# Turnings of attention rows, norm steps, spare banks and gates placed anew in a chain of two fused networks

## What is computed

```python
def rmsnorm(x, g):
    return x * rsqrt(mean(x * x, axis=-1) + EPS) * g

# mix: 8 heads of 64, 512 rows in blocks of 128
s = einsum('bhqd,bkhd->bhqk', q_i, k) * scale + cq_i[..., None] - c[:, :, None, :]
p = softmax(where(mask, s, -inf), axis=-1)
y_att = einsum('bhqk,bkhd->bqhd', p, v)
x = x + concat([rmsnorm(y_conv, g_conv_out), rmsnorm(y_att, g_att_out)]) @ w_mix_out

# x: 4 heads of 256, 256 memory rows
q = rmsnorm(x, g_xattn) @ w_q
k, v = split(rmsnorm(mem, g_mem) @ w_kv, 2)
x = x + attention(q, k, v) @ w_o

# last stage: 16 heads of 64
z = einsum('bhqd,bhsd->bhqs', q, k) * scale
suffix = cumsum(log_sigmoid(-z) * mask, axis=3, reverse=True) - log_sigmoid(-z) * mask
a = where(mask, exp(log_sigmoid(z) + suffix), 0)
o = einsum('bhqs,bshe->bhqe', a, v)
x = x + (o * silu(g)) @ w_out
```

## Time and profile before

| | us |
|---|---|
| median of 3 runs | 2913.24 |
| lowest and highest | 2910.73, 2915.46 |
| profiled execution | 2911.05 |
| its span | 2909.2 |
| PE busy | 2843.3 |
| DVE busy | 1676.3 |
| ACT busy | 1092.2 |
| POOL busy | 397.3 |
| mean granted clock of PE | 0.995 |

### The profile page before, as it was taken

How to read it: one execution, slowest core, us unless ns; L and a number is a source line. 1 busy time by engine, 2 the same in 40 slices (tenths; PEclk the granted TensorE clock), 3 DMA queues, 4 the chain that set the end, 5 groups by cost and what they waited for, 6 DMA issues and landing times.

```text
span 2909.2 us, 34967 instructions
## 1 busy us (share of the span) xinstructions
PE 2843.3 (98%) x14241; PEld 2363.5 (81%) x14241; DVE 1676.3 (58%) x2400; ACT 1092.2 (38%) x1699; POOL 397.3 (14%) x263
## 2 busy tenths in 40 slices
PE   8999999999999999999999999999999899899988
PEld 7888887888888888888887889888888787678777
DVE  5554357675464533555247776555533677768884
ACT  4322244554332322323234454422222444444442
POOL 2000111110100001000011220100001322154430
PEclk9999999999999999999999999999999999999999
DMA  4332332243233233332323233233323222131211
GB/s 141 101 95 94 95 88 73 66 127 106 87 94 97 88 101 98 101 95 87 105 71 92 68 108 118 80 109 95 101 91 98 70 64 69 47 88 59 72 59 51
DMA packets 302240, 258.08 MB, mean 89 GB/s; under 512 B 11367, under 2 KB 299904, under 8 KB 302080
## 3 DMA queue, kind: packets, MB, share of 16 engines
q1 hardware_dynamic: 300704, 254.76, 28.7%
q10 hardware_dynamic: 1024, 1.05, 0.2%
q0 software_dynamic: 352, 0.03, 0.0%
HBM read 252.66 MB, written 2.10 MB: 88 GB/s over the span
## 4 chain that ended last, share of the span: by engine, by line
PE 82%; DVE 10%; ACT 3%; issue 3%; POOL 2%; DMA 1%; ACTq 0%; SPq 0%; POOLq 0%; DVEq 0%
PE PS L1525 26%; PE PS L1527 25%; PE PS L1526 25%; DVE WL L2255 3%; PE PS L1531 2%; PE PS L1770 1%; DVE AF L2701 1%; DVE SM L2619 1%; ACT AF L2129 0%; PE PS L1623 0%; PE PS L1812 0%; PE PS L1811 0%; DVE AR L2711 0%; ACT WH L1872 0%; POOL SM L2869 0%
## 5 line engine op out<-in xcount | busy, mean ns | idle before, releaser
L2255 DVE TENSOR_TENSOR WL<-RAW,WH 128x1024 fp32r<-128x1024 f32 x480 | 617.9, 1293 | 572.9 <-ACT WH L1872 572.6
L1525 PE MATMUL PS<-XH,WL 128*128 128x512 f32 x2256 | 904.4, 401 | 2.9 <-DVE XL L2265 2.9
L1527 PE MATMUL PS<-XH,WH 128*128 128x512 f32 x2256 | 883.3, 392 | 0.0
L1526 PE MATMUL PS<-XL,WH 128*128 128x512 f32 x2256 | 882.1, 391 | 0.0
L1872 ACT ACTIVATE WH<-RAW 128x1024 fp32r<-128x1024 f32 x448 | 465.4, 1044 | 1005.9 <-PE PS L1527 994.6
L1525 PEld LDWEIGHTS PS<-XH,WL 128*128 128x128 f32 x2256 | 425.8, 189 | 101.5 <-issue 12.7
L1527 PEld LDWEIGHTS PS<-XH,WH 128*128 128x128 f32 x2256 | 425.2, 188 | 91.5
L1526 PEld LDWEIGHTS PS<-XL,WH 128*128 128x128 f32 x2256 | 426.3, 189 | 81.1
L1525 PE MATMUL PS<-AR,WL 128*128 128x512 f32 (+1 forms) x1216 | 465.3, 383 | 7.3 <-DVE SC L2599 3.5
L1527 PE MATMUL PS<-AR,WH 128*128 128x512 f32 (+1 forms) x1216 | 460.7, 379 | 0.0
L1526 PE MATMUL PS<-AR,WH 128*128 128x512 f32 (+1 forms) x1216 | 460.6, 379 | 0.0
(11 more groups left out here) (259 smaller groups left out, 3000.0 us busy)
## 6 DMA issues: line engine op xcount, KB each, us to landing
RAW<-in_w_ffn_gu_dram SPq DMA_DIRECT2D x176, 512.0 KB, 3.5
RAW<-in_w_ffn_down_dram SPq DMA_DIRECT2D x80, 512.0 KB, 3.4
RAW<-in_w_mix_in_dram SPq DMA_DIRECT2D x48, 512.0 KB, 4.0
RAW<-in_w_xkv_dram SPq DMA_DIRECT2D x32, 512.0 KB, 3.4
RAW<-in_a_w_in_dram SPq DMA_DIRECT2D x32, 512.0 KB, 4.2
RAW<-in_w_mix_out_dram SPq DMA_DIRECT2D x16, 512.0 KB, 3.4
RAW<-in_w_xq_dram SPq DMA_DIRECT2D x16, 512.0 KB, 4.1
RAW<-in_w_xo_dram SPq DMA_DIRECT2D x16, 512.0 KB, 3.4
```

The source lines that it names most:

```text
L1525: pe.matmul(o, ll, rh, start=start, stop=False, skip_group_check=skip)
L1526: pe.matmul(o, lh, rl, start=False, stop=False, skip_group_check=skip)
L1527: return pe.matmul(o, lh, rh, start=False, stop=stop, skip_group_check=skip)
L2255: dve.tensor_tensor(l, raw_slot(n), F(h), ALU.subtract).then_inc(sg["wl"].up(n))
```

## The change

Four things are placed anew; no arithmetic changes.

1. *Rows.* In `att` of mix and of the last stage there is no break between the turning of a row and the scores that follow it, as long as there are scores (n < 16, n < 32). The rates of the side streams are lower accordingly, as they now count fewer and larger steps.
2. *Mix.* The second half of the first values goes to bank 7 instead of the next in turn.
3. *x.* `norm_a` stands behind 12 steps of the first queries' tile instead of 10, `norm_b` behind 5 steps of the second keys instead of 2. The output projection takes its first two pairs of banks in the order in which they come in turn.
4. *Last stage.* `norm_a` stands 3 steps into the tile q1, `norm_b` 3 steps into k1, which gets a bank of its own and is finished before the rows start. Gate 6 moves from `opening` into block t=7.

```diff
@@ mix, att @@
                     self.add("bt", (s, m), "ptr", "ph")
-                    yield
+                    if n >= 16:
+                        yield
@@ mix @@
-        self.drain(self.flow(self.values(s, 0)))
+        self.drain(self.flow(self.values(s, 0, 7)))
-        side = self.stream(att(0, 4), 6.5 / 64)
+        side = self.stream(att(0, 4), 4.3 / 64)
-            side = self.stream(att(4 * m, 4 * m + 4), 10.5 / 80)
+            side = self.stream(att(4 * m, 4 * m + 4), 6.3 / 80)
-        side = self.stream(att(12, 16), 10.5 / 80)
+        side = self.stream(att(12, 16), 6.3 / 80)
-        side = self.stream(att(16, 19), 4.5 / 44)
+        side = self.stream(att(16, 19), 4.4 / 54)
@@ x, second_keys @@
-            for _ in range(2):
+            for _ in range(5):
                 yield next(g)
             self.norm_b(s)
@@ x @@
         g = self.flow(queries(0))
-        for _ in range(10):
+        for _ in range(12):
             next(g)
         self.norm_a(s)
...
+        a, b, c, d = self.turn
         self.own_banks(4, 5)
-        self.out_proj(s, self.stream(att(3), 8.2 / 48), flow=True)
+        self.out_proj(s, self.stream(att(3), 8.2 / 48), ((a, b), (c, d)), flow=True)
@@ out_proj @@
-        ch = {p: out(p, 2 * p) for p in range(4)}
+        ch = {p: out(p, bb) for p, bb in enumerate((*pairs, (4, 5), (6, 7)))}
@@ values @@
-            b = self.take()
+            b = self.take() if spare is None or n == 0 else spare
@@ last stage, att @@
                     self.later(5, "btl", (s, m), "pl")
-                    yield
+                    if n >= 32:
+                        yield
@@ last stage @@
+        g = self.tile(q1, b1)
+        for _ in range(3):
+            next(g)
         self.norm_a(s)
-        g = self.tile(q1, b1)
-        for _ in range(6):
+        self.drain(g)
+        kb = self.take()
+        g = self.tile(((s, "k1"), 0), kb)
+        for _ in range(3):
             next(g)
         self.norm_b(s)
-        self.drain(g)
...
-        side = self.stream(att(0, 4), 6 / 64)
-        self.weave(self.flow(self.chain(qk("k", 1), self.values(s, 0), gated(0))), side)
+        self.drain(self.flow(g))
+        self.give(kb, "bql", (s, "k", 1))
+        self.heads_in(s, "k", 1)
+        side = self.stream(att(0, 4), 4.3 / 48)
+        self.weave(self.flow(self.chain(self.values(s, 0), gated(0))), side)
...
-            if t < 7:
-                main.append(gated(t - 1))
-            side = self.stream(att(4 * t - 4, 4 * t), 10.5 / (32 + (32 if t % 2 else 0) + (16 if t < 7 else 0)))
+            main.append(gated(t - 1))
+            side = self.stream(att(4 * t - 4, 4 * t), 6.3 / (48 + (32 if t % 2 else 0)))
...
-            yield from self.chain(gated(6), gated(7))
+            yield from gated(7)
             yield from self.mm(out[0], range(0, 6))
-        side = self.stream(att(28, 33), 13 / 56)
+        side = self.stream(att(28, 33), 8.2 / 40)
```

More of the change, by code:

```diff
@@ L758, in xattn, with out_proj @@
             self.finish(side)
+        a, b, c, d = self.turn
         self.own_banks(4, 5)
-        self.out_proj(s, self.stream(att(3), 8.2 / 48), flow=True)
-    def out_proj(self, s, side, flow=False):
+        self.out_proj(s, self.stream(att(3), 8.2 / 48), ((a, b), (c, d)), flow=True)
+    def out_proj(self, s, side, pairs, flow=False):
         def out(p, bb):
-            return self.chunk((s, f"o{p}"), (bb, bb + 1), "o", [("x", (s + 1, 2 * p + c)) for c in range(2)])
+            return self.chunk((s, f"o{p}"), bb, "o", [("x", (s + 1, 2 * p + c)) for c in range(2)])
         def close(p):
             self.resid(s, (2 * p, 2 * p + 1), ((ch[p], 0), (ch[p], 1)))
-        ch = {p: out(p, 2 * p) for p in range(4)}
+        ch = {p: out(p, bb) for p, bb in enumerate((*pairs, (4, 5), (6, 7)))}
         g = self.mm_two(ch[0], ch[1])
@@ L1040, in heads_in, with values @@
         self.later(6, "bql", (s, w, t), "el")
-    def values(self, s, c):
+    def values(self, s, c, spare=None):
         ch = ((s, f"v{c}"), 0)
         for n in range(2):
-            b = self.take()
+            b = self.take() if spare is None or n == 0 else spare
             yield from self.rows_tile(ch, n, b, (lambda: self.add("evh", (ch, 1), "vh")) if n else lambda: None)
```

## The result

| | before | after |
|---|---|---|
| median of 20 runs each | 2912.84 | 2917.49 |
| lowest and highest | 2908.67, 2915.89 | 2914.37, 2919.90 |
| span of the profiled execution | 2909.2 | 2916.4 |
| its mean granted clock | 0.995 | 0.991 |

The ratio is 1.0015, with a 95% interval of 1.0009 to 1.0021. I had forecast 2903.4, with a range of 2889 to 2914. The measured time is outside the range and on the other side of no change.

What follows compares the result with a forecast made beforehand. TensorE, busy 98% with a fixed matmul order, bounds the kernel, so only its waits and low clock count. Last stage 4.8, mix 2.8 and cross attention 2.2 make 9.8 off 2911.05: 2901.25, as a median 2903.4, range 2889 to 2914.

Steps and rivals of the forecast that it cites:

- Mix, the spare bank: Mix, second half of the first values: a bank of its own removes a wait of 1.01 for bank 0, +1.0.
- Mix, the first product of the last rows: Mix, last block of rows: its first product comes later and loses some 0.5 of 0.65 waiting, +0.5 (0 to 0.7).
- Mix, the end: End of mix's rows: old waits (1.48, 2.08) go, an equally long new one comes, -0.1 net (-1 to +1.5).
- Cross attention: Cross attention, twice: the norm's wait of 0.96 is covered, the output projection starts 0.16 earlier; together +1.1 per layer.
- Last stage, opening: Start of the last stage: one wait of some 1.9 at the values' first tile replaces two totalling 2.4, +0.5.
- Row 2: Last stage, t=2: turning late by 0.8 from three fewer steps, more if a GpSimd scaling runs late; -3.5 (-0.8 to -4.9).
- Rows 6 and 14: Last stage: one more step before the turning gains 0.68, but VectorE scales a q tile ahead (0.7): 0.
- Rows 10 and 18: Last stage: one more step cuts lateness to 2.0, gaining 0.68 plus 1.7 of clock: +2.4 each.
- Row 22: Last stage: three more steps, part given to a scaling; lateness 3.06 becomes 1.7 and the clock stays: +3.0.
- The end: Last rows and first output steps: moved gate +4.9, longer row 26 wait -3.5, shorter spacings -1.4: 0 (-3.5 to +3.5).
- The clock: PE's waits anywhere: a wait costs its length below 2.4, and 1.7 more from 2.67 through half clock.
- Rival C: Slower: uneven turning spacing lets GpSimd go first and makes turnings late at six places; 2926, milder 2920; chance 13%.

Runs made afterwards that it cites:

- a1: Changed kernel with one low part of weights ahead of the residual adds in mix, and two last-stage scalings behind row 3's multiplication: 2903.50 in one traced execution.
- a2: Changed kernel with three side-stream rates altered (last of mix, first and last but one of the last stage): 2904.90 in one traced execution.
- d1: Kernel before the change, with only the low part of weights in mix moved ahead of the residual adds: 2917.00 in one traced execution.

## Why the prediction was wrong, point by point

- **Mix, the spare bank, +1.0 per layer.** Wrong: 0 to 1.0 in the first layer, 0 in the second. I carried one row to both layers. No group of mine showed that wait in the second layer, and there was none.
- **Mix, the first product of the last rows, +0.5.** Right: its wait of 0.65 is gone in both layers.
- **Mix, the end, -0.1 (to -1).** This step failed most of all there. The trade of old waits for new ones as such was right (1.48 and 2.08 gone; an output step late by 1.86, and 2.98 at the memory rows for 0.71), but I had priced the new ones at the length of the old. I followed the moved turnings to PE's and DVE's work and not on to SP: the turning of row 15 holds back a low part of weights, that holds a buffer, and that the load of the second memory row. Together with the clock, which I had not counted in mix at all, mix came out at -2.2 and -2.3 instead of +1.4. a1 and a2 take it away in two independent ways.
- **Cross attention, +1.1 per layer.** Right: 1.2. The norm's 0.96 went whole, and the output's wait of 1.67 became one of 1.49 at the next bank.
- **Last stage, opening, +0.5.** Right: 1.62 in place of 2.4.
- **Row 2, -3.5 (to -4.9).** This is the term that failed most in the last stage. The mechanism was right, the size too small: 6.15, and 3.3 of clock, 9.5 in all. I allowed one scaling to be late; POOL ran both, 5.01, since it waited for the transfer. I also left the scans at their undisturbed length, and took the chain from scores to turning as unchanged, where its scans start 2.0 later. a1 shows that the scalings made half of it, a2 that four steps of distance take away all but a product's 1.70.
- **Rows 6 and 14, 0.** Wrong to the good side: their waits of 1.7 and 1.8 went, +3.5. Why the tile scaled ahead did not eat the added step I did not look into.
- **Rows 10 and 18, +2.4 each.** The lateness fell further than forecast, to 1.53, but the next turning and the next product, which I had not followed, became late by 1.09 and 1.50: 4.1 in place of 2.7. With the clock's 1.7 kept, some +0.3 each.
- **Row 22, +3.0.** Its wait went whole, with its fall of the clock: +4.8.
- **The end, 0 (to -3.5).** Late by 3.54 at row 26, where I had 4.2, but 2.66 at row 29, where I had 0.7 of shorter spacing, and 4.5 of clock for 1.7 before. Waits and clock are 13.2 against 9.3: -3.9, just beyond my bound. At row 29 the low part of row 28 stands in VectorE's order behind L2745, which waits for ScalarE:

```profile
2861.42 0.69 DVE L2745 TENSOR_TENSOR AR<-AF,AR 128x512 fp32r<-128x512 f32 x1 [3.24 <-ACT AR L2196]
2862.14 0.42 DVE L2720 TENSOR_TENSOR AR<-PS,AR 128x256 fp32r<-128x256 f32 x1
```

- **The clock, 1.7 from 2.67 on and nothing below 2.40.** Wrong as a rule: seven waits of one execution that happened to fit. d1, with the same last stage, breaks it at 1.50, 2.37 and 2.67.

By these the last stage comes to 0.7 - 9.5 + 3.5 + 0.6 + 4.8 - 3.9 = -3.8, measured -4.2; 0.4 of it stays unassigned. Rival C had the sign and two of the places, t=2 and the end, but its own mechanism showed at two places only, rows 11 and 19 (1.09 each), not at six, and its 2920 to 2926 lie above the measured 2917.49. So what failed is the term for the end of mix (2.2 and 2.3 lost where 1.4 was to be won), the size of row 2 (9.5 for 3.5), the new waits behind rows 10 and 18, and the clock as a fixed price. The range was too narrow because two of its bounds, at the end of mix and at row 2, left out what a late transfer does, and because the clock had none at all.

## What to carry to other kernels

When a hand-placed order is moved, follow each moved step over every queue up to the transfers: the costliest effects here were one low part of weights behind eight adds, which held back a load by 5 us, and two scalings ahead of a multiplication. Parts that gain when tried alone (3.0, 5.1 and 7.4) can lose together (4.2), so time each alone and then in pairs, stage by stage in the trace, and read waits and clock apart: of these gains only 1.0, 0.5 and 4.0 were waits. A lead won upstream is worth nothing if a step that holds back the next load has no lead: here the 2.3 that PE had won were lost at the memory rows.

## What was unexpected of the hardware

The granted clock of PE falls to half for 3.4 us, or for 5.4 to 6.8 us behind some waits of 2.9 to 6.2, but not by a fixed length of wait: it fell behind 1.50 and stayed behind 2.67, 2.68 and 3.03, and it changed between two executions of the same kernel. A difference of 1 to 2 us per fall, and of up to 3 us in two parts whose code did not change, stands beside any reading of single waits.
